# Splitting a streamed weight tile into its two parts in one instruction per engine instead of two

## The reference

```python
qa, ka, va, qb, kb, vb = jnp.split(h @ w_in, cuts, axis=-1)
...
xr, g = jnp.split(h @ w_in, 2, axis=-1)
...
a = jnp.maximum(h @ w1, 0)
return (a * a) @ w2
...
m = jax.nn.silu(cond) @ w + b
```

## Time and profile before

| | us |
|---|---|
| three runs | 2509.2, 2510.1, 2514.39 |
| median | 2510.1 |
| span of the profiled execution, first to last instruction | 2507.5 |
| TensorE busy (matmul) | 2356.4 |
| VectorE busy | 1492.8 |
| ScalarE busy | 1107.1 |

### The profile page before, as it was taken

One profiled execution on the slowest core, in us unless ns is written; L12 is line 12 of the kernel. 1 busy time (PEld: TensorE's weight loads), 2 busy tenths in 40 slices (PEclk: granted clock), 3 DMA queues, 4 the chain that ended last, 5 costly groups with the idle time before them and its releaser, 6 DMA issues.

```text
span 2507.5 us, 34322 instructions
## 1 busy us (share of the span) xinstructions
PE 2356.4 (94%) x12179; PEld 1818.1 (73%) x12179; DVE 1492.8 (60%) x2055; ACT 1107.1 (44%) x1529; POOL 85.9 (3%) x139
## 2 busy tenths in 40 slices
PE   5799997989999999999998999897999999999996
PEld 1366765668888887877876777665888888777775
DVE  2444445456555556666767668865655556666665
ACT  0132334334333334555554358733444444555553
POOL 1000000000000000000000011000000000000000
PEclk8799998989999999999999999998999999999998
DMA  9989880765777777666674887687455555766763
GB/s 355 330 299 323 308 316 5 276 227 189 252 251 252 250 251 258 225 250 214 223 251 150 304 285 246 240 284 274 152 189 184 196 186 178 258 220 212 249 218 117
DMA packets 296342, 592.14 MB, mean 236 GB/s; under 512 B 11569, under 2 KB 11825, under 8 KB 296017
## 3 DMA queue, kind: packets, MB, share of 16 engines
q1 hardware_dynamic: 289744, 574.77, 65.5%
q0 software_dynamic: 6528, 16.46, 2.1%
HBM read 587.76 MB, written 3.42 MB: 236 GB/s over the span
## 4 chain that ended last, share of the span: by engine, by line
PE 86%; DMA 5%; DVE 4%; ACT 2%; issue 1%; POOL 1%; DVEq 0%; SPq 0%; ACTq 0%; POOLq 0%
PE bank L539 22%; PE bank L529 15%; PE bank L531 14%; PE bank L530 14%; PE bank L541 11%; PE bank L494 6%; DMA raw<-in_w_ada 3%; PE bank L644 1%; PE bank L556 1%; PE bank L678 1%; DMA raw<-in_w_rec_in 1%; DVE w_lo L1027 1%; DVE x L1154 1%; DMA raw<-in_w_att_in 1%; POOL small L405 0%
## 5 line engine op out<-in xcount | busy, mean ns | idle before, releaser
L1027 DVE TENSOR_TENSOR w_lo<-raw,w_hi 128x1024 fp32r<-128x1024 f32 x712 | 858.0, 1221 | 512.4 <-ACT w_hi L776 511.0
L776 ACT ACTIVATE w_hi<-raw 128x1024 fp32r<-128x1024 f32 x712 | 734.0, 1051 | 725.9 <-DMA raw<-in_w_att_in 217.9
L539 PE MATMUL bank<-xt,w_hi 128*128 128x512 f32 x2560 | 907.5, 399 | 4.0 <-DVE R L1047 2.5
L541 PE MATMUL bank<-xt,w_lo 128*128 128x256 f32 x2560 | 713.4, 279 | 0.0
L529 PE MATMUL bank<-w_hi,xt 128*128 128x512 f32 x1568 | 624.9, 399 | 11.8 <-DVE w_lo L1027 4.1
L531 PE MATMUL bank<-w_hi,xt 128*128 128x512 f32 x1568 | 612.1, 390 | 0.0
L530 PE MATMUL bank<-w_lo,xt 128*128 128x512 f32 x1568 | 611.7, 390 | 0.0
L539 PEld LDWEIGHTS bank<-xt,w_hi 128*128 128x128 f32 x2560 | 480.4, 188 | 159.2 <-issue 31.9
L541 PEld LDWEIGHTS bank<-xt,w_lo 128*128 128x128 f32 x2560 | 481.9, 188 | 0.4
L529 PEld LDWEIGHTS bank<-w_hi,xt 128*128 128x128 f32 x1568 | 294.9, 188 | 150.5 <-issue 66.5
L531 PEld LDWEIGHTS bank<-w_hi,xt 128*128 128x128 f32 x1568 | 295.0, 188 | 63.4
(11 more groups left out here) (171 smaller groups left out, 916.1 us busy)
## 6 DMA issues: line engine op xcount, KB each, us to landing
raw<-in_w_ff SPq DMA_DIRECT2D x256, 1024.0 KB, 5.4
raw<-in_w_ada SPq DMA_DIRECT2D x192, 1024.0 KB, 5.6
raw<-in_w_att_in SPq DMA_DIRECT2D x36, 1024.0 KB, 7.0
raw<-in_w_rec_in SPq DMA_DIRECT2D x32, 1024.0 KB, 7.0
raw<-in_w_att_out SPq DMA_DIRECT2D x16, 1024.0 KB, 7.2
raw<-in_w_rec_out SPq DMA_DIRECT2D x16, 1024.0 KB, 7.2
gain_rows<-in_g_post_mix POOLq DMA_DIRECT2D x8, 256.0 KB, 5.0
gain_rows<-in_g_post_ffn POOLq DMA_DIRECT2D x8, 256.0 KB, 4.1
```

The source lines that it names most:

```text
L539: nc.tensor.matmul(ps[m][:, :], w_hi[:, h, k, m * P:(m + 1) * P], xt[:, c, :], start=(begin and k == 0), stop=False)
L541: mm = nc.tensor.matmul(ps[m][:, 0:NG * T], w_lo[:, h, k, m * P:(m + 1) * P], xt[:, c, 0:NG * T], start=False, stop=(end and k == 1))
L776: nc.scalar.activation(w_hi[:, h % NSPLIT, :, :], raw[:, slot, 2 * q:2 * q + 2, :], ACT.Copy)\
L1027: V.tensor_tensor(w_lo[:, h % NSPLIT, :, :], raw[:, slot, 2 * q:2 * q + 2, :], w_hi[:, h % NSPLIT, :, :].bitcast(fp32), ALU.subtract).then ...
```

## The change

A call of `split` with an even half now does both halves of the tile, and a call with an odd half does nothing. ScalarE waits until both places of the ring are free (`half_used` one higher), copies the whole tile in one instruction of 128x2048, and counts `hi_ready` up by 2; VectorE waits for both, subtracts the whole tile in one instruction and counts `lo_ready` up by 2. In ff2 the activations of the tile, four chunks, go the same way, as 128x1024. The wait for `hidden_ready` in ff2's first block asks for two chunks more. `NSPLIT`, the four `raw` slots, TensorE's and SyncE's programs and all else stay as they are. A `split_early` call for one odd half thus does nothing, and one for an even half does the tile.

```diff
@@ ScalarE
             def split(s, it, h):
+                if h % 2:
+                    return
                 n = s.half0 + it * s.halves + h
-                t, q = divmod(h, 2)
+                t = h // 2
...
                     if first(it):
-                        act.wait_ge(hidden_ready, hidden0[s.name] + 2 * h + 2)
-
-                if q == 0:
-                    act.wait_ge(raw_landed[slot], landed)
+                        act.wait_ge(hidden_ready, hidden0[s.name] + 2 * h + 4)
+
+                act.wait_ge(raw_landed[slot], landed)
                 if not isinstance(n, int) or n >= NSPLIT:
-                    act.wait_ge(half_used, n - NSPLIT + 1)
+                    act.wait_ge(half_used, n - NSPLIT + 2)
                 if s.tiles == 16:
                     c = 2 * h % KC
-                    nc.scalar.activation(xt[:, c:c + 2, 0:NG * T], hidden[:, 2 * h:2 * h + 2, :], ACT.Copy)
-                nc.scalar.activation(w_hi[:, h % NSPLIT, :, :], raw[:, slot, 2 * q:2 * q + 2, :], ACT.Copy)\
-                    .then_inc(hi_ready, 1)
+                    nc.scalar.activation(xt[:, c:c + 4, 0:NG * T], hidden[:, 2 * h:2 * h + 4, :], ACT.Copy)
+                nc.scalar.activation(w_hi[:, h % NSPLIT:h % NSPLIT + 2, :, :],
+                                     raw[:, slot, :, :].rearrange("p (q k) n -> p q k n", q=2), ACT.Copy)\
+                    .then_inc(hi_ready, 2)
@@ VectorE
             def split(s, it, h):
+                if h % 2:
+                    return
...
-                dve.wait_ge(hi_ready, n + 1)
+                dve.wait_ge(hi_ready, n + 2)
                 if s.tiles == 16:
                     c = 2 * h % KC
-                    V.tensor_tensor(xt[:, c:c + 2, NG * T:2 * NG * T], hidden[:, 2 * h:2 * h + 2, :],
-                                    xt[:, c:c + 2, 0:NG * T].bitcast(fp32), ALU.subtract)
-                V.tensor_tensor(w_lo[:, h % NSPLIT, :, :], raw[:, slot, 2 * q:2 * q + 2, :],
-                                w_hi[:, h % NSPLIT, :, :].bitcast(fp32), ALU.subtract).then_inc(lo_ready, 1)
+                    V.tensor_tensor(xt[:, c:c + 4, NG * T:2 * NG * T], hidden[:, 2 * h:2 * h + 4, :],
+                                    xt[:, c:c + 4, 0:NG * T].bitcast(fp32), ALU.subtract)
+                V.tensor_tensor(w_lo[:, h % NSPLIT:h % NSPLIT + 2, :, :],
+                                raw[:, slot, :, :].rearrange("p (q k) n -> p q k n", q=2),
+                                w_hi[:, h % NSPLIT:h % NSPLIT + 2, :, :].bitcast(fp32), ALU.subtract).then_inc(lo_ready, 2)
```

## The result

The changed kernel takes 2587.34 us (median of four runs, 2579.87 to 2591.59); the kernel before, run beside it, 2509.65 us (2506.16 to 2514.39). The ratio is 1.0302, 95% interval 1.0287 to 1.0317: slower by 78 us. The prediction, 2563 in a range of 2540 to 2590, has the sign and holds the time, 24 us under it. The profiled execution took 2591.59 us with a span of 2589.9, 82.4 more than the span before. Of all executions in this document one, the fourth of whole_in_ff2, was slow, 2724.62 us at a mean granted clock of 0.83 where the others have 0.92 to 0.97; it is in that run's median and not in its ratio.

The account below looks back on a forecast made before the run. It took TensorE to be the bound, held up if split tiles come late. 42 (ff2) + 3.5 (early splits) + 2.5 and 0.8 (recurrence) + 4 (landings) = 53 us on 2510: 2563, range 2540 to 2590.

Parts of the forecast that it names:

- What bounds the kernel: Whole kernel: TensorE holds 86% of the chain; ScalarE and VectorE busy time matters little, split tiles being ready in time does.
- Durations: Whole-tile instructions at 1.89 us on ScalarE and 2.28 on VectorE; ff2's activations at 1.05 and 1.22.
- The slope: Cost per element from two instruction sizes: 0.82 ns on ScalarE, 1.04 ns on VectorE, used to size the merged instructions.
- The round trip in ff2: End of tile t-2 to start of tile t: 6.54 us against 5.28 available, 1.26 lost per pair; ff2 +42 us.
- the signs it named: New profile: L529 waits for w_lo 50 to 90 times, some 40 us, nearly all in ff2; no such L539 waits in ff1_1.
- The first pair of either ff2 sweep: Start of ff2_0 and ff2_1: prepared while ff1 ends, so about 2 us taken off the ff2 loss.
- Residual and early splits: Between sweeps, VectorE's early split does a whole tile ahead of the residual; four such places, +3.5 us.
- Landings: Where a weight landing is on the chain, TensorE waits 1.9 us longer; one of either counted, +4, maybe 0 or 10.
- The recurrence: rec_in_b: ScalarE's longer copy delays feature_out by 0.85 at three blocks and the flush, +2.5; rec_out's last early tile, +0.8.
- ff1_1: No activation copies: round trip 4.4 us inside a stretch of 5.38, so nothing lost, no waits for w_lo.
- The lower clock: Rival: waits drop TensorE to 1.2 GHz in the 64 pure tiles, 5.44 us more each, over 2800; chance 0.02.
- The rival at 2587: Landings also bind in the adaLN half of ff2 blocks, about 1 us at three pairs in eight blocks, +24; chance 0.07.

Follow-up runs that it names:

- whole_in_ff2: Whole-tile split of the changed kernel in the two ff2 sweeps only, halves of the kernel before in all others; 2560.2 us, ratio 1.0192.
- gates_whole: Kernel before, instructions still in halves, but with the changed kernel's waits for a whole tile on ScalarE and TensorE; 2528.52 us, ratio 1.0071.
- after_again: The changed kernel, unaltered, run once more; 2590.29 us, ratio 1.0302 against the kernel before.
- hidden_ahead: Changed kernel with the ff2 activations split one tile ahead, behind the present tile's weights, on both engines; 2541.51 us, ratio 1.0127 against the kernel before.
- scalar_whole: Kernel before with ScalarE doing the whole tile in one instruction, VectorE still in halves, TensorE free to start on half a tile; 2541.41 us, ratio 1.012.
- vector_whole: Kernel before with VectorE doing the whole tile in one instruction, ScalarE still in halves, TensorE getting both halves at once; 2553.13 us, ratio 1.0171.
- halves_in_ff2: Changed kernel with halves put back in the two ff2 sweeps, whole tiles in all others; 2538.51 us, ratio 1.0102 against the kernel before.
- halves_ff2_rec: Changed kernel with halves put back in ff2 and the three recurrent sweeps, whole tiles in attention and ff1; 2524.18 us, ratio 1.0059 against the kernel before.
- copy_extra: Changed kernel plus an unused ScalarE 128x512 copy ahead of each tile's activations in three of four blocks of either ff2 sweep; 2614.04 us, ratio 1.0406.

## Why the prediction was right, and where its terms were off

- **What bounds the kernel**: right. ScalarE and VectorE gave 115 us of busy time back and the time rose by 78. The rule of the Trainium skill, "Perfetto Trace Analysis", section "Optimizing Scalar/DVE Operations", that breaking up such instructions may let work finish sooner, has the sign of what was measured; the Trainium skill's "VectorE: DVE Perf Modes", section on the TRN2 errata, that a large tile pays the fixed latency once, is also borne out (the two halves of the earlier trace rows took 2.36, the whole takes 2.28), but what that saves is busy time, which was not the bound.
- **Durations**: 1.89, 2.28, 1.05 and 1.22 predicted, 1.909, 2.289, 1.059 and 1.225 measured. The slope held.
- **The round trip in ff2**: 6.54 predicted, 6.49 measured. Each pair of tiles loses it once, as said: in the steady blocks the four pairs without an adaLN tile add 1.28, 1.31, 1.14 and 1.35 us, those with one 0.05 to 0.17 each (0.17 predicted). A steady block adds 5.2 to 5.5, predicted 5.5. Of the signs it named, L529 waits 52 times (50 to 90 predicted) but only 32.0 us (some 40): a pair's loss is mostly spread over both its tiles, and idle time shows less than is lost.
- **The first pair of either ff2 sweep**: wrong. The prediction took 2 us off, "prepared while ff1 ends". It costs 1.9 and 2.6 instead, with 1.6 more at the tile after in ff2_1, the stretch at the lower clock. The timeline of all engines of the kernel after, at the start of ff2_1:

```profile
2169.91 2.28 DVE L1031 TENSOR_TENSOR w_lo<-raw,w_hi 128x2048 fp32r<-128x2048 f32 x1
...
2171.12 0.28 PE L541 MATMUL bank<-xt,w_lo 128*128 128x256 f32 x1
...
2172.11 0.41 DVE L1052 TENSOR_TENSOR R<-bank,R 128x256 f32<-128x256 f32 x1
...
2174.49 0.41 DVE L1052 TENSOR_TENSOR R<-bank,R 128x256 f32<-128x256 f32 x1
...
2175.05 0.47 PE L529 MATMUL bank<-w_hi,xt 128*128 128x512 f32 x1 [3.65 <-DVE R L1052]
```

  and before:

```profile
2115.38 0.47 PE L529 MATMUL bank<-w_hi,xt 128*128 128x512 f32 x1 [1.02 <-DVE R L1047]
```

  The tile was indeed split in time. But VectorE's list has the last output of ff1, four times L1052, behind that split, and TensorE waits for the last of the four: 3.65 us, 1.02 before. The early tile stands in the way of the work that ends the sweep. With this ff2 adds 48.2, against 42.
- **Residual and early splits** (+3.5): right where it was worked out: from the last gate multiply to the update of x ahead of rec_in_a it is 1369.97 to 1374.05, 4.08 us, against 1336.87 to 1339.70 before, 1.25 more (1.2 predicted). The places together show 2.6 (1.1 ahead of rec_in_a, 1.2 in ff1_0, 0.3 ahead of ff1_1); the 1.2 in ff1_0 comes from a wait of L539 in the fourth tile for normed activations (L1182), a place that was not priced.
- **Landings** (+4, "may be 0 or 10"): undersized. "One of either" was counted; in att_in alone TensorE waits three times for w_lo, 6.3 us together (once, 2.4 us, before), and with its start att_in adds 8.7, of which 2.7 by the lower clock. The size varies: the six profiles with this att_in add 5.1 to 9.2.
- **The recurrence** (+2.5 and +0.8): undersized. The one wait that was priced is right (L539 for `feature_out`: the earlier trace rows had 1.26, after has 2.04 at the same block, 0.78 more for 0.85), though three block starts and the flush at 0.85 are 3.4, not 2.5. But beside rec_out's start (0.8, as measured) it was the only one priced: the starts of the sweeps, rec_in_a's tiles and rec_out's later tiles were counted at nothing, and rec_in_a to rec_out add 16.1. That halves give all of it back is shown; how it splits among landings, written order and the lower clock (some 3.9) was not taken apart further.
- **ff1_1** (0): no wait for w_lo, as predicted, and still 7.6 us. Some 6.5 of it are pace, the last section's matter (0.105 a tile; gates_whole, which has the pace and no wait there, adds 6.5). The rest is a wait for normed activations in the fourth tile (L1182, 0.9 us of idle), as in ff1_0; before has none there.
- **The lower clock** (a rival's, at over 2800): not in the tiles that the rival named, but some 8 us elsewhere, which no term had.

So 24 us under: the terms for the steady part of ff2 held, the breaks in it were counted too few, and neither the pace nor the clock was in the sum. That the range holds the time is in part luck: its upper end stood for a merging that saves nothing and 10 us of landings, and breaks, pace and clock filled it instead; after_again, with 2590.29, lies just past it. The rival at 2587 names the very time, but its mechanism, landings that bind in the half of an ff2 block with adaLN tiles, is not what happened: that half adds 0.05 to 0.17 us a pair.

## What to carry to other kernels

Before merging instructions that fill a ring, add up the whole loop from the release of a place to its next use, all engines in series, and set it beside the time the consumer takes for the other places; saved instruction starts (here 115 us of busy time) are worth nothing if the loop gets longer than that. Then count every place where the steady run breaks (start and end of a sweep, a last tile that waits for all its parts, work behind a split in a written list, a late landing): there the larger piece can be paid in full, and they cost some 32 us here, beside 44 in the ff2 sweeps and 6.5 by TensorE's pace; some 8 of these 82 are not waits but the lower clock behind long ones. If large instructions are wanted, first take out of the loop what needn't be in it, as hidden_ahead did with the activations.

## What the hardware did that was not expected

TensorE has two paces for the same alternation of 128x512 and 128x256 matmuls, with no wait and a granted clock of 1.00 in both. From a tile's first matmul to the next tile's first, over 32, they come 173.3 ns apart in ff1_1 in the profile of before, hidden_ahead, whole_in_ff2, scalar_whole and vector_whole, and 176.7 in that of after, after_again, gates_whole, halves_in_ff2, halves_ff2_rec and copy_extra. The windows of 100 us in ff1_1 (us, busy us and count of PE, PEld, DVE, ACT, POOL, then clock, DMA share, GB/s), first of before:

```profile
1940.00:2040.00 100.00, 100.00 (x578) 87.40 (x578) 57.49 (x69) 43.59 (x53) 0.00 (x0) 1.00 0.58 189
```

of after:

```profile
1990.00:2090.00 100.00, 100.00 (x569) 86.75 (x568) 54.72 (x57) 40.01 (x35) 0.00 (x0) 1.00 0.58 188
```

and of hidden_ahead, whose ff1_1 is the program of after:

```profile
1970.00:2070.00 100.00, 100.00 (x579) 88.15 (x578) 53.57 (x51) 40.41 (x37) 0.00 (x0) 1.00 0.59 189
```

578, 569 and 579 matmuls: the size of the splits doesn't decide it, and neither does the DMA traffic. Both paces occur in one execution: the timeline of TensorE in ff1_0 of before, first and last matmul of two tiles, each the second behind an adaLN tile:

```profile
855.73 0.39 PE L539 MATMUL bank<-xt,w_hi 128*128 128x512 f32 x1
...
861.16 0.28 PE L541 MATMUL bank<-xt,w_lo 128*128 128x256 f32 x1
...
868.12 0.40 PE L539 MATMUL bank<-xt,w_hi 128*128 128x512 f32 x1
...
873.66 0.28 PE L541 MATMUL bank<-xt,w_lo 128*128 128x256 f32 x1
```

From first to last, 31 steps, it is 5.43 us in the one and 5.54 in the other, 12 us later. In ff1_0, where adaLN tiles stand between, the pace changes at such a tile; in ff1_1, which has none, it holds from its first tiles to the end. What sets it was not found. Single runs of one kernel that lie some 8 us apart (2580 and 2588 of after) would fit it, but only profiled runs show the pace.
